# A PEER encoder block on one core: eight more dot products beside each tile's selections, one fewer per scatter turn, pairs chosen from 112 candidates

## The reference, cut to what matters

```python
s_top, i_top = lax.top_k(s, K)                       # K = 16, over 128 keys, for each head and side
cand = (s_top[..., 0, :, None] + s_top[..., 1, None, :]).reshape(B, L, PEER_HEADS, K * K)
best, flat = lax.top_k(cand, K)
i1 = jnp.take_along_axis(i_top[..., 0, :], flat // K, axis=-1)
i2 = jnp.take_along_axis(i_top[..., 1, :], flat % K, axis=-1)
expert = i1 * PEER_NKEYS + i2
gate = jax.nn.softmax(best.astype(jnp.float32), axis=-1)
...
act = jax.nn.gelu(jnp.einsum('ld,lkd->lk', xb, u_tab[e]), approximate=False)
return jnp.einsum('lk,lkd->ld', act * g, v_tab[e])
```

## Time and profile before

| What | Value |
|---|---|
| median of three runs | 2871.51 us |
| profiled execution, its own time | 2873.07 us |
| its span, first to last instruction | 2871.3 us |
| retrieve, from the first scores to the last block's end (windows 1568 to 1897) | some 330 us |
| spread loop on VectorE | 1904 to 2196 us |
| busy over the span | PE 87%, VectorE 62%, GpSimd 43%, ScalarE 31% |
| granted TensorE clock, mean | 0.949 |

### The profile page before, as it was taken

One profiled execution on the slowest core, in us unless ns is written; L12 is line 12 of the kernel. 1 busy time (PEld: TensorE's weight loads), 2 busy tenths in 40 slices (PEclk: granted clock), 3 DMA queues, 4 the chain that ended last, 5 costly groups with the idle time before them and its releaser, 6 DMA issues. The chain is left out here.

```text
span 2871.3 us, 43150 instructions
## 1 busy us (share of the span) xinstructions
PE 2503.2 (87%) x14285; PEld 1409.1 (49%) x14285; DVE 1771.6 (62%) x3539; ACT 900.6 (31%) x1357; POOL 1232.4 (43%) x744
## 2 busy tenths in 40 slices
PE   5999998967999999988989899978888698888885
PEld 3344343435677766675434455545555233333332
DVE  6123122027676666753331798889997688888886
ACT  4212212123323333222223333334443233333332
POOL 3312313213122122212323577666565576777764
PEclk9999999988999999999989999999999899999998
DMA  5201201121000000002231588768989899999994
GB/s 184 88 29 58 88 29 66 52 84 45 8 29 22 29 29 29 7 0 85 78 126 49 166 266 285 246 223 314 350 325 354 280 310 310 315 317 316 315 312 144
DMA packets 192978, 456.84 MB, mean 159 GB/s; under 512 B 17664, under 2 KB 100224, under 8 KB 192784
## 3 DMA queue, kind: packets, MB, share of 16 engines
q1 hardware_dynamic: 149136, 296.59, 29.6%
q0 software_dynamic: 36864, 134.23, 14.6%
q10 hardware_dynamic: 6912, 25.17, 2.2%
HBM read 403.50 MB, written 52.43 MB: 159 GB/s over the span
## 5 line engine op out<-in xcount | busy, mean ns | idle before, releaser
L1760 POOL TENSOR_TENSOR hid_u_lo<-hid_u,hid_u_hi 128x1024 bf16<-128x1024 f32 x128 | 292.9, 2289 | 228.8 <-ACT hid_u_hi L1744 228.4
L2373 PE MATMUL bank<-ex_v_hi,ex_gated_hi 128*128 128x512 bf16 x768 | 301.4, 392 | 85.4 <-DVE ex_gated_lo L2431 73.4
L148 PE MATMUL bank<-hT_hi,hid_u_hi 128*128 128x384 bf16 x1024 | 337.6, 330 | 39.2 <-POOL hid_u_lo L1760 28.3
L2411 POOL TENSOR_TENSOR ex_v_lo<-ex_v,ex_v_hi 128x1024 bf16<-128x1024 f32 x128 | 274.3, 2143 | 153.8 <-ACT ex_v_hi L2395 153.7
L148 PE MATMUL bank<-hT_lo,hid_u_hi 128*128 128x384 bf16 x1024 | 337.2, 329 | 0.0
L148 PE MATMUL bank<-hT_hi,hid_u_lo 128*128 128x384 bf16 x1024 | 336.9, 329 | 0.0
L203 POOL TENSOR_TENSOR ret_w_lo<-ret_w_raw,ret_w_hi 128x1024 bf16<-128x1024 f32 x72 | 153.0, 2162 | 401.4 <-ACT ret_w_hi L198 401.4
L2373 PE MATMUL bank<-ex_v_hi,ex_gated_lo 128*128 128x512 bf16 x768 | 300.3, 391 | 0.0
L2373 PE MATMUL bank<-ex_v_lo,ex_gated_hi 128*128 128x512 bf16 x768 | 299.3, 390 | 0.0
L2438 DVE SCALAR_TENSOR_TENSOR wide<-ex_row,row_gated,wide 128x1024 f32<-128x1024 f32 x128 | 164.4, 1284 | 17.2 <-DMA ex_row<-in_peer_v,row_index 16.9
L2397 ACT ACTIVATE ex_gated_hi<-ex_gated 128x384 bf16<-128x384 f32 x128 | 66.9, 522 | 343.0 <-DVE ex_gated L2428 343.0
(11 more groups left out here) (486 smaller groups left out, 5785.7 us busy)
## 6 DMA issues: line engine op xcount, KB each, us to landing
hid_u<-in_peer_u SPq DMA_DIRECT2D x128, 512.0 KB, 5.5
ex_v<-in_peer_v SPq DMA_DIRECT2D x128, 512.0 KB, 6.1
ret_w_raw<-in_w_ret SPq DMA_DIRECT2D x60, 512.0 KB, 4.2
expert_hidden<-hid_gelu SPq DMA_DIRECT2D x128, 192.0 KB, 4.5
expert_weights<-spread_grid ACTq DMA_DIRECT2D x48, 512.0 KB
ex_gated<-expert_hidden SPq DMA_DIRECT2D x128, 192.0 KB, 4.6
ex_weights<-expert_weights SPq DMA_DIRECT2D x64, 384.0 KB, 5.8
dn_w_raw<-in_w_dn SPq DMA_DIRECT2D x36, 512.0 KB, 3.3
```

Of the source, the lines that this page charges most:

```text
L148: last = nc.tensor.matmul(out, left[l], right[r], start=start and i == 0, stop=stop and i == len(PASSES) - 1)
L1760: self.nc.gpsimd.tensor_tensor(self.us[1][:, m % 2, :, :], self.u32[:, m % RING, :, :], self.us[0][:, m % 2, :, :], ALU.subtract).then_inc ...
L2373: last = nc.tensor.matmul(bank[:, :], gs[l][:, slot, t * P:(t + 1) * P], vs[r][:, slot, half * 512:(half + 1) * 512], start=j == 0 and i == 0,
L2411: nc.gpsimd.tensor_tensor(vs[1][:, n % 8, :], v32[:, n % RING, :], vs[0][:, n % 8, :], ALU.subtract).then_inc(s["v_lo"], 1)
```

## The change

Three edits go together. Per tile 24 instead of 16 dots lie beside the selections: the 16 calls now take one or two each, and GpSimd issues three rows behind two blocks (after block j the tile's first 3j/2+2, rounded down), up to block 16. In a scatter turn two dots instead of three are done (after slots 0 and 1), rows go through eight slots, and one row is gathered behind each block. So 72 dots come before the scatter loop, 48 in it and 8 behind it. The best pairs are chosen from 112 candidates: all 16 partners of the first four, and the first four partners of the other twelve; nine more instructions turn the position among the 112 into two ranks. The scatter's number table (`iota`) is loaded into the output grid instead of a buffer of its own, and two semaphores of an earlier stage are used again, with their counts.

```diff
--- before.py
+++ after.py
@@ -1665,8 +1667,8 @@
 TILES = (NT - 1,) + tuple(range(NT - 1))
 SHARES = (12, 20, 20, 20)
 PICKS = PH * TOPK
-BESIDE_TILE = 16
-BESIDE_TURN = 3
+BESIDE_TILE = 24
+BESIDE_TURN = 2
 SPAN = 64
 AHEAD = 2
...
+    LONG, SHORT = 4, 4
+    WIDE = LONG * TOPK
+    CAND = WIDE + (TOPK - LONG) * SHORT
+    assert (LONG + 1) * (SHORT + 1) > TOPK
...
-        pairs = sbuf(nc, ctx, "top_pairs", [P, PH, TOPK, TOPK])
+        pairs = sbuf(nc, ctx, "top_pairs", [P, PH, CAND])
+        spare = work[:, 0:PH * CAND].rearrange("p (h c) -> p h c", h=PH)
         left = work[:, :].rearrange("p (h a b) -> p h a b", h=PH, a=TOPK)
...
@@ -1974,8 +1985,8 @@
                     for n in range(ends[s], ends[s + 1]):
                         hidden.split_lo(pool, n, n)
                         j = n - ends[s]
-                        while s and 1 <= j < BESIDE_TILE and \
-                                k < min((s - 1) * BESIDE_TILE + j + 1 + AHEAD, (NT - 1) * BESIDE_TILE):
+                        while s and 1 <= j <= SHARES[s] - RING and \
+                                k < min((s - 1) * BESIDE_TILE + 3 * j // 2 + AHEAD, (NT - 1) * BESIDE_TILE):
                             gathered.gather(pool, k)
                             k += 1
...
-                    step(nc.vector.tensor_tensor(pairs[:, :, :, :], by_head[:, :, 0, :].unsqueeze(3).broadcast_to(wide),
-                                                 by_head[:, :, 1, :].unsqueeze(2).broadcast_to(wide), ALU.add))
-                    best_of(pairs[:, :, :, :].rearrange("p h a b -> p h (a b)"),
-                            left[:, :, :, :].rearrange("p h a b -> p h (a b)"), PH, top, topi)
-
-                    nc.vector.tensor_scalar(rank[:, 0, :, :], topi[:, :, :], 4, None, ALU.logical_shift_right)
-                    link(nc.vector.tensor_scalar(rank[:, 1, :, :], topi[:, :, :], 15, None, ALU.bitwise_and))
-                    link(nc.vector.tensor_copy(rankf[:, :, :, :], rank[:, :, :, :]))
-
-                    link(nc.vector.tensor_copy(total[:, :], top[:, :, 0]))
+                    for at, a0, a1, n in ((0, 0, LONG, TOPK), (WIDE, LONG, TOPK, SHORT)):
+                        some = [P, PH, a1 - a0, n]
+                        ins = nc.vector.tensor_tensor(
+                            pairs[:, :, at:at + (a1 - a0) * n].rearrange("p h (a b) -> p h a b", b=n),
+                            by_head[:, :, 0, a0:a1].unsqueeze(3).broadcast_to(some),
+                            by_head[:, :, 1, 0:n].unsqueeze(2).broadcast_to(some), ALU.add)
+                    step(ins)
+                    best_of(pairs, spare, PH, top, topi)
+
+                    for dst, shift in ((rank, 4), (short, 2)):
+                        nc.vector.tensor_scalar(dst[:, 0, :, :], topi[:, :, :], shift, None, ALU.logical_shift_right)
+                        ins = nc.vector.tensor_scalar(dst[:, 1, :, :], topi[:, :, :], 2 ** shift - 1, None,
+                                                      ALU.bitwise_and)
+                    nc.vector.tensor_scalar(is_short[:, :, :], topi[:, :, :], float(WIDE), None, ALU.is_ge)
+                    link(ins)
+                    nc.vector.tensor_copy(rankf[:, :, :, :], rank[:, :, :, :])
+                    nc.vector.tensor_copy(total[:, :], top[:, :, 0])
+                    link(nc.vector.tensor_copy(shortf[:, :, :, :], short[:, :, :, :]))
+                    link(nc.vector.tensor_scalar(shortf[:, 0, :, :], shortf[:, 0, :, :], float(LONG - WIDE // SHORT),
+                                                 None, ALU.add))
+                    link(nc.vector.tensor_tensor(shortf[:, :, :, :], shortf[:, :, :, :], rankf[:, :, :, :],
+                                                 ALU.subtract))
+                    for side in range(2):
+                        ins = nc.vector.tensor_tensor(shortf[:, side, :, :], shortf[:, side, :, :], is_short[:, :, :],
+                                                      ALU.mult)
+                    link(ins)
+                    link(nc.vector.tensor_tensor(rankf[:, :, :, :], rankf[:, :, :, :], shortf[:, :, :, :], ALU.add))
                     nc.vector.tensor_tensor(top[:, :, :], top[:, :, :],
                                             total[:, :].unsqueeze(2).broadcast_to([P, PH, TOPK]),
                                             ALU.subtract).then_inc(exp_arg, 1)
@@ -2065,11 +2093,13 @@
                 with dve.Fori(0, NT - 1) as later:
-                    order = iter(range(BESIDE_TILE))
+                    order, calls = iter(range(BESIDE_TILE)), iter(range(16))
 
                     def beside():
-                        j = next(order)
-                        gathered.dot(dve, later * BESIDE_TILE + j, later * (16 * BESIDE_TILE // RING), j, j)
+                        call = next(calls)
+                        for _ in range(BESIDE_TILE * call // 16, BESIDE_TILE * (call + 1) // 16):
+                            j = next(order)
+                            gathered.dot(dve, later * BESIDE_TILE + j, later * (16 * BESIDE_TILE // RING), j, j)
 
                     tile(later + 1, beside)
                     gathered.keep(dve, later * BESIDE_TILE, BESIDE_TILE, later + 1)
...
-    ring = RING + 2
+    ring = 2 * RING
     with ExitStack() as ctx:
-        iota = sbuf(nc, ctx, "spread_iota", [P, NK])
...
+        iota = grid[:, 0, 0:NK // SPAN, :].rearrange("p k t -> p (k t)")
+        iota_in = core.spent_loads[1]
...
@@ -2263,7 +2294,7 @@
                 k = dots_before + RING
                 for n in range(blocks, BLOCKS):
                     hidden.split_lo(pool, n, n)
-                    for _ in range((1, 2)[n % 2] if n < blocks + busy else 1):
+                    for _ in range(BESIDE_TURN // 2 if n < blocks + busy else 1):
                         if k < PICKS:
                             gathered.gather(pool, k, dots_before)
                             k += 1
```

More of the change, by code:

```diff
@@ L122, in __init__ @@
         self.products = [0] * 8
+        self.spent_loads = []
     def sem(self, name):
@@ L244, in embed @@
         x_in = [core.sem(f"embed_x_in{t}") for t in range(NT + 1)]
+        core.spent_loads += x_in
         gb_in, shift_ready, normed = core.sem("embed_gb_in"), core.sem("embed_shift"), core.sem("embed_normed")
@@ L1868, in retrieve @@
         rank = sbuf(nc, ctx, "top_rank", [P, 2, PH, TOPK], U32)
+        short = sbuf(nc, ctx, "top_short", [P, 2, PH, TOPK], U32)
+        shortf = sbuf(nc, ctx, "top_short_f", [P, 2, PH, TOPK])
+        is_short = sbuf(nc, ctx, "top_is_short", [P, PH, TOPK])
         rankf = sbuf(nc, ctx, "top_rank_f", [P, 2, PH, TOPK])
@@ L1872, in retrieve @@
         chosen = sbuf(nc, ctx, "top_chosen", [P, 3, PH, TOPK])
-        keys_in, dve_steps, exp_arg, exp_ready, chosen_ready, turned = (
-            core.sem("top_" + n) for n in ("keys_in", "dve_steps", "exp_arg", "exp_ready",
+        keys_in = core.spent_loads[0]
+        dve_steps, exp_arg, exp_ready, chosen_ready, turned = (
+            core.sem("top_" + n) for n in ("dve_steps", "exp_arg", "exp_ready",
                                            "chosen_ready", "turned"))
@@ L1906, in _ @@
                         qb.fills(f"q{c}", last)
-                pe.wait_ge(keys_in, 32)
+                pe.wait_ge(keys_in, 16 + 32)
                 for c in range(4):
@@ L1986, in _ @@
                 dve.wait_ge(exp_arg, 1)
-                dve.wait_ge(keys_in, 32)
+                dve.wait_ge(keys_in, 16 + 32)
                 def tile(t, beside):
-                    link = Chain(dve, dve_steps, 0, t, 18)
+                    link = Chain(dve, dve_steps, 0, t, 21)
                     def step(ins):
@@ L2105, in spread @@
         grid = sbuf(nc, ctx, "spread_grid", [P, 2, NK, SPAN])
-        iota_in, dve_steps, first_ready, second_ready, place_ready = (
-            core.sem("spread_" + n) for n in ("iota_in", "dve_steps", "first_ready", "second_ready", "place_ready"))
+        iota = grid[:, 0, 0:NK // SPAN, :].rearrange("p k t -> p (k t)")
+        iota_in = core.spent_loads[1]
+        dve_steps, first_ready, second_ready, place_ready = (
+            core.sem("spread_" + n) for n in ("dve_steps", "first_ready", "second_ready", "place_ready"))
         stored = [core.sem(f"spread_stored{side}") for side in range(2)]
@@ L2128, in _ @@
             def _(sp):
-                sp.dma_start(iota[:, :], a["iota"]).then_inc(iota_in, 16)
+                sp.dma_start(iota, a["iota"]).then_inc(iota_in, 16)
                 def store_and_load(n, m):
@@ L2158, in _ @@
                                           picked[:, 1 + key, 0:DENSE].unsqueeze(2).broadcast_to(copies))
-                dve.wait_ge(iota_in, 16)
-                link(nc.vector.tensor_copy(numbers[:, :], iota[:, :]))
+                dve.wait_ge(iota_in, 16 + 16)
+                link(nc.vector.tensor_copy(numbers[:, :], iota))
                 with dve.Fori(0, DENSE // TURN // RING) as four:
```

## The result

The kernel after takes 2876.18 us (median of 10 runs, 2872.40 to 2879.69), the kernel before 2869.99 (10 runs) beside it: ratio 1.0019, 95% interval 1.0010 to 1.0028. In a second set it was 2868.55 (12 runs) against 2870.16 (29 runs): ratio 0.9996, 0.9986 to 1.0007. So the change is within 0.3%: 6 us more in one set, none in the other. The forecast was 2884, 12.5 us more than before. Its direction doesn't survive the second set, and two of its terms were wrong, in opposite directions.

A forecast was written before the change was run, and what follows sets the result against it. VectorE was taken to bound the scatter loop and TensorE the tiles' bodies. From 2873.1 us, -5 (first tile), +27.6 (three tiles) and -9.4 (scatter) gave 2886.3, 2884.7 against the median, stated as 2884; range 2861 to 2899.

The forecast's parts named there:

- What bounds the kernel now: Scatter loop bound by VectorE, tile bodies by TensorE; Exp operand 4.9 us early in the third tile, late in the first.
- the operand's 4.9 us: Third tile: VectorE's Exp operand was ready 4.9 us before ScalarE took the Exp.
- First tile: Retrieval's first tile, without dots: cheaper selection brings the Exp operand 4.9 us sooner, 5 us gained (4.6 to 6.8).
- Eight more dots a tile: Tiles two to four: a late last row delays operand and next scores, 9.2 us longer each, 27.6 in all.
- GpSimd's shift of +0.5 us: In a tile, two rows behind every second block delay block 15's remainder on GpSimd by some 0.5 us.
- One dot less a scatter turn: Scatter loop: a turn falls from 12.16 to 11.77 us, 9.4 us gained over 24 turns (5 to 27.6).
- nearly free: Scatter loop: a dot under GpSimd's remainder fills time in which builds stand anyway; the removed dot is this one.
- slot 3's builds stand the full 1.94: Scatter turn: without the third dot, slot 3's builds stall the full 1.94 us under GpSimd's remainder.
- if the stalls stay as they are: Scatter loop's upper bound: the removed dots gain their full price of 1.15 us each, 27.6 us.
- The sum: Whole kernel: 2873.1 - 5 + 27.6 - 9.4 = 2886.3 us, 2884.7 against the median, stated as 2884.
- the rival of that name: Whole kernel: a tile costs 5.7 us, scatter gains 9.4, first tile 6.8, giving 2872 us; chance 0.08.
- one with a single SBUF input doesn't contend: Rule cited for the scatter loop: only VectorE instructions with two SBUF inputs contend with a GpSimd instruction reading SBUF.

The follow-up runs named there:

- the candidates alone: The kernel before with only the pair selection over 112 candidates changed, 16 dots a tile and three a scatter turn kept: 2873.20 us, ratio 1.0007.
- the ring of six: The kernel after with six row slots in the retrieval's tiles and rows issued up to five ahead of their dots: 2854.94 us, ratio 0.9947.

## Why the prediction was wrong

*What bounds the kernel now.* Right, with one gap: the operand's 4.9 us were not free in tiles two to four. With the candidates alone the operand came 3.0 to 3.6 us later against GpSimd there, still in time, and a tile cost 2.3 us more, through the collision, which the forecast had no term for.

*First tile.* Right: -5 forecast, -5.5 measured in every kernel with 112 candidates but the two that move the Exp or halve the lookups; ScalarE waited 1.08 us instead of 4.64.

*Eight more dots a tile.* The chain was right step by step, and its pieces close: the last row's issue to its dot 7.0 forecast and 7.4 seen, ranks 3.3 and 3.3, Exp late 6.2 and 6.05, scores behind Exp 20.3 and 20.4. The size was low: 9.2 us a tile against 11.3 to 12.1 in the mean, 27.6 against 33.8 to 36.3 in all. The term mis-sized is GpSimd's shift of +0.5 us ahead of block 15's remainder. In the third tile it began 65.3 us behind the scores' start instead of 62.5, that is +2.8, where TensorE paused in the body (1.69 us once in the third tile) and GpSimd stood 13.5 us for free places over the three tiles, 5.6 before.

*One dot less a scatter turn.* This is the step that failed: the removed dot as "nearly free", and "slot 3's builds stand the full 1.94" in each turn, 9.4 us gained in all. Measured were 24.4 and 29.6 us, around what I had as the upper end, 27.6, "if the stalls stay as they are". They did, in sum: each build's time above 0.41 us, added over the loop, makes 3.28 us a turn before and 3.41 and 3.08 in the two profiles of after, where the forecast has 3.88. So VectorE's loop became shorter by about the price of its dots, 291.9 to 267.3 and 258.7 us:

```profile
1931.55 0.43 DVE L2200 TENSOR_TENSOR spread_place<-spread_numbers,spread_keys_of 128x512 bf16<-128x512 bf16 x1 [0.36 <-DVE spread_numbers L2191]
...
2198.85 0.21 DVE L1832 TENSOR_SCALAR row_dots<-row_fresh 128x8 f32 x1
```

Two things were wrong in the step. The 0.86 and 1.94 of the earlier trace rows were read rightly, but as a turn's stalls before they make 2.80, and with them a turn's parts sum to 11.84 us and not to the 12.16 measured: that pair of half turns isn't the mean one. And I took the remainder's place against the dots as fixed. With the dots after slots 0 and 2 it nearly is, and there the forecast holds (stalls of 3.97 us a turn, 9.9 us gained). In the kernel after it isn't: in part of the turns a remainder is held until a dot comes, the builds then stand 0.80 instead of 1.94, and VectorE's 16 builds, two dots, keep and two such stalls (5.44 + 2.30 + 0.15 + 1.60 = 9.5 us, an estimate from these rows) fit under TensorE's two blocks of 4.8, which with a third dot they would not. Then VectorE is no longer the bound and the place stays. A run of 12 builds isn't needed for it: with the dots after slots 1 and 3 the runs are of 8, and fast stretches come as well.

*The sum.* Both misses cancel in part: 15 to 20 us more gained in the loop, 6 to 9 lost in the tiles. That the first set lies on the forecast's side of no change is luck: with the tiles' 27.6 and the loop's gain as measured the kernel would have been 2 to 8 us faster than before by the stages. The edits cancel, but for another reason than the rival of that name gave (a tile of 5.7 us). From the stages alone, -5.5 + 36.3 - 24.4 makes +6.4 and -5.5 + 33.8 - 29.6 makes -1.3; the two sets' medians differ from before by +6.2 and -1.6. So close a fit is chance too: the profiled executions, from which the stages are read, differ from the profiled before by -0.2 and -4.0, the rest lying outside the stages.

*Left open.* Why the remainder of 2042.98 is let in at 2043.31 and that of 2089.58 is held: both start 0.01 us behind a build's start and 3.2 us behind a dot's. Block 90's was let in in one profile of after and held in the other, 3.1 us behind a dot in both. No run here tells what decides. Nor is it shown what the 3 us behind the loop are.

## What to carry to other kernels

Where two engines exclude each other, as GpSimd's remainder and VectorE's builds do here, an instruction's price is set by what lies under the other's instruction, and how the two lie can differ from turn to turn. Price both ways, and take the stalls from the whole loop and not from two half turns. Try the uncontended work where the other engine's instruction begins: inside slots 1 and 3 it gave 7 us in the median against before. When a transfer feeds the last step before a handover, issue and free slot must both be early: the deeper ring with earlier issue gave back 20 of 36 us, the earlier issue alone 4 to 6. And look twice before cutting a long instruction on a path that ends a stage: here the halves let the other engine in twice where the whole let it in once, and the kernel lost 10 us.

## What the runs showed of the hardware

GpSimd can stand through a run of short VectorE instructions: the remainder at 2089.58 was ready while five more builds began, 0.34 us apart and none stalled, and by its length got its turn only under the dot, 2 us later. In the other direction a build stands for what is left of the remainder, up to 1.94 us. Instructions with one SBUF input were caught as well, so the prediction's sentence that one with a single SBUF input doesn't contend is too wide; it holds for the dot and the reductions here. With the candidates alone and with the ring of six, VectorE:

```profile
1782.18 1.97 DVE L2051 TENSOR_SCALAR top_rank<-top_of_pairs_index 128x128 uint32<-128x128 uint32 x1
```

```profile
1790.33 2.10 DVE L2060 COPY top_total<-top_of_pairs 128x8 f32<-128x8 f32 x1
```

Each begins with or behind a remainder (1781.94 and 1790.27) and takes 2 us instead of 0.2 (as the row at 1802.31 above; the copy 0.16 in the kernel after), while the reductions over 2048 elements took 2.28 or 2.29 us in all fourteen profiles, beside a remainder or not.
